# Attention units of a one-core fp32 kernel: VectorE's rescale ahead of the maximum, and masked key blocks left out

## What is computed

```python
# first model, layer 0: four heads of "differential" attention, q and k of 64, v of 128
w = probs(q1b, k1) - lam * probs(q2b, k2)          # softmax(where(causal, s, -inf))
o = einsum('bqhk,bkhd', w, v)
# first model, layer 0: four "forget" heads, a decay added to each score
s = q @ k + cum_logf[query] - cum_logf[key]
o = softmax(where(causal, s, -inf)) @ v
# first model, layer 1: eight heads, three dilated windows (128,1), (512,4), (2048,16),
# merged by their log-sums: one softmax with log(how many patterns hold the key) added
# second model, layer 0: eight query heads over 256 tokens + 256 context keys, no mask
p = softmax(q @ concat(k, k_ctx)); o_ctx = softmax(q_ctx @ k_ctx) @ v_ctx
# second model, layer 1: sixteen heads, blocks of 128 queries
in_window = abs(key - query) <= 128                # of 256 tokens; beyond the edges: no key
s_win = where(in_window & exists, q @ k, -1e30)
p = softmax(concat(s_win, q @ k_ctx, sink))[..., :-1]
```

## Time and profile before

| | |
| --- | --- |
| median of the runs | 2828.0 us (3 runs, 2827.4 to 2834.32) |
| the profiled execution | 2829.54 us, its span 2827.8 us |
| TensorE busy | 2536.1 us, 90% of the span |
| VectorE busy | 1515.0 us, 54% |
| ScalarE busy | 891.9 us, 32% |
| GpSimd busy | 76.5 us, 3% |
| mean granted TensorE clock | 0.951 of full speed |
| DMA | 110 GB/s mean |

### The profile page before, as it was taken

The page is one execution under the profiler, slowest core; times in us unless marked ns, Lnnn a source line. Parts: engine busy times, 40 slices in busy tenths (PEclk is TensorE's granted clock), DMA queues, the critical chain, the costliest instruction groups (busy, mean ns, idle before and its releaser), DMA issues.

```text
span 2827.8 us, 41887 instructions
## 1 busy us (share of the span) xinstructions
PE 2536.1 (90%) x17518; PEld 2006.7 (71%) x17518; DVE 1515.0 (54%) x2517; ACT 891.9 (32%) x1547; POOL 76.5 (3%) x148
## 2 busy tenths in 40 slices
PE   8999999799997899548886899998999997888998
PEld 6687778588875567248773588876788875556998
DVE  5656475555554655674543555545555543664554
ACT  2331131422222333712220422223322223343543
POOL 0000000000000000000000000000000000000000
PEclk9999999999998999779998999999999998999999
DMA  7235436243433110000011243443344441101553
GB/s 285 82 118 200 172 121 220 99 142 135 148 134 136 60 45 31 0 2 4 4 39 52 84 147 137 141 149 119 129 139 142 142 143 69 43 30 45 175 184 134
DMA packets 55770, 309.72 MB, mean 110 GB/s; under 512 B 5920, under 2 KB 9376, under 8 KB 28064
## 3 DMA queue, kind: packets, MB, share of 16 engines
q1 hardware_dynamic: 32944, 224.74, 22.2%
q0 software_dynamic: 20736, 75.51, 8.0%
q10 hardware_dynamic: 1904, 6.80, 0.6%
HBM read 305.98 MB, written 1.05 MB: 109 GB/s over the span
## 4 chain that ended last, share of the span: by engine, by line
PEld 39%; PE 31%; issue 12%; DVE 11%; ACT 7%; DMA 1%; PEldq 0%; DVEq 0%; ACTq 0%; SPq 0%
PEld bank L1206 13%; PEld bank L1199 13%; PEld bank L1202 12%; PE bank L1079 4%; PE bank L1258 4%; PE bank L1076 2%; PE bank L1052 2%; PE bank L1138 2%; PE bank L1154 2%; PE bank L943 2%; PE bank L950 2%; PE bank L946 2%; ACT hn L1567 2%; PEld bank L910 1%; PE bank L1033 1%
## 5 line engine op out<-in xcount | busy, mean ns | idle before, releaser
L1991 DVE TENSOR_TENSOR w_lo<-ring,w_hi 128x1024 fp32r<-128x1024 f32 (+1 forms) x198 | 236.2, 1193 | 450.6 <-ACT w_hi L1532 450.6
L1202 PE MATMUL bank<-ffn_x_lo,w_hi 128*128 128x512 f32 x1008 | 399.6, 396 | 0.0
L1206 PE MATMUL bank<-ffn_x_hi,w_lo 128*128 128x512 f32 x1008 | 399.6, 396 | 0.0
L1199 PE MATMUL bank<-ffn_x_hi,w_hi 128*128 128x512 f32 x1008 | 399.6, 396 | 0.0
L1532 ACT ACTIVATE w_hi<-ring 128x1024 fp32r<-128x1024 f32 (+1 forms) x198 | 203.7, 1029 | 290.2 <-PE bank L1202 278.6
L1923 DVE SCALAR_TENSOR_TENSOR ms<-mod_rows,c_silu 128x1024 f32<-128x1024 f32 x200 | 243.9, 1220 | 1.2
L1206 PEld LDWEIGHTS bank<-ffn_x_hi,w_lo 128*128 128x128 f32 x1008 | 189.9, 188 | 46.3
L1199 PEld LDWEIGHTS bank<-ffn_x_hi,w_hi 128*128 128x128 f32 x1008 | 189.9, 188 | 46.3
L1202 PEld LDWEIGHTS bank<-ffn_x_lo,w_hi 128*128 128x128 f32 x1008 | 189.8, 188 | 46.3
L1199 PE MATMUL bank<-ffn_h_hi,w_hi 128*128 128x512 f32 x528 | 211.7, 401 | 0.0
L1206 PE MATMUL bank<-ffn_h_hi,w_lo 128*128 128x512 f32 x528 | 209.3, 396 | 0.0
(11 more groups left out here) (430 smaller groups left out, 4642.8 us busy)
## 6 DMA issues: line engine op xcount, KB each, us to landing
ring<-in_stream SPq DMA_DIRECT2D x211, 1024.0 KB, 4.8
mod_rows<-in_mod_stream POOLq DMA_DIRECT2D x144, 512.0 KB, 3.8
one_const<-in_one ACTq DMA_DIRECT2D x1, 1665.0 KB, 14.2
mix_const<-in_two ACTq DMA_DIRECT2D x1, 1440.0 KB, 6.2
win_const<-in_win ACTq DMA_DIRECT2D x1, 1089.0 KB, 5.4
x<-in_x SPq DMA_DIRECT2D x4, 256.0 KB, 4.5
c_silu<-in_c SPq DMA_DIRECT2D x1, 1024.0 KB, 10.3
x<-in_x SPq DMA_DIRECT2D x1, 1024.0 KB, 26.5
```

Of the source, the lines that this page charges most:

```text
L1199: mm = pe.matmul(bank[:, 0:tok], w_high, hi, start=k == 0, stop=False)
L1202: mm = pe.matmul(bank[:, 0:tok], w_high, lo, start=False, stop=False)
L1206: mm = pe.matmul(bank[:, 0:tok], w_low, hi, start=False, stop=last)
L1991: V.tensor_tensor(low[:, 0:h.nk, :], raw_half(h), high[:, 0:h.nk, :].bitcast(F32), ALU.subtract).then_inc(sem("w_split"), 1)
```

## The change

It has two parts.

**Key blocks left out.** Units of the first query block (t=0) of the differential, forget and dilated forms now have 128 keys for each part and not 256: half of the score columns, two transposes for four, half of the product matmuls. Window units leave out the block of keys beyond the edge that all of them had in their 512 columns: they have 384. The causal mask is added only on the block of 128 keys on the diagonal (`mask_at`), the window mask only on the 128 token keys that it can shut out in part, the dilated one on all keys that are kept. It is added in place, in PSUM; the tile `s` is not written, the maximum and the exponential read PSUM, and so it is ScalarE that frees the bank, after the exponential, and signals `exp_ready` by an instruction behind that. ScalarE's copy of the transposed probabilities is as wide as the unit.

**VectorE's order.** `step(i)` of VectorE's attention is split into `largest(i)` (mask, maximum, sink, sign) and `rescaled(i)` (the rescale of unit i-1). Where a step follows something other than a unit, `fresh`, `rescaled(i)` comes first: in the mixers always, in the blends in the first step of each group of two or four. In the others the order is as before.

```diff
-                    def step(i):
+                def largest(i):
                     if i < n:
                         u = us[i]
                         bank, free = full_bank()
-                        src = bank[:, 0:u.width]
+                        src = bank[:, 0:u.width].rearrange("p (k w) -> p k w", k=u.parts)
                         if u.mask is not None:
-                            src = u.bufs["s"][:, i % 2, 0:u.width]
-                            link(V.tensor_tensor(src, bank[:, 0:u.width], u.mask, ALU.add))
-                            dve.nop().then_inc(free, 1)
-                        link(V.tensor_reduce(stats[:, i % 4, 0:u.parts], src.rearrange("p (k w) -> p k w", k=u.parts),
-                                             AX_X, ALU.max))
+                            part = src[:, :, u.mask_at:u.mask_at + u.mask.shape[2]]
+                            link(V.tensor_tensor(part, part, u.mask, ALU.add))
+                        link(V.tensor_reduce(stats[:, i % 4, 0:u.parts], src, AX_X, ALU.max))
...
+                def rescaled(i):
                     if 1 <= i < n + 1:
                         u = us[i - 1]
...
+                def step(i, fresh):
+                    if fresh:
+                        rescaled(i)
+                        largest(i)
+                    else:
+                        largest(i)
+                        rescaled(i)
...
 # ScalarE, exponential and copy
-                            src = (u.bufs["s"][:, i % 2, :] if u.mask is not None else psum[b])[:, k * w:(k + 1) * w]
-                            last = nc.scalar.activation(u.bufs["p"][:, i % 3, k * w:(k + 1) * w], src, ACT.Exp,
+                            last = nc.scalar.activation(u.bufs["p"][:, i % 3, k * w:(k + 1) * w], psum[b][:, k * w:(k + 1) * w], ACT.Exp,
...
-                        if u.mask is None:
-                            last.then_inc(bank_free[b], 1)
-                            act.wait_ge(bank_free[b], use + 1)
-                            act.nop().then_inc(sem("exp_ready"), 1)
-                        else:
-                            last.then_inc(sem("exp_ready"), 1)
+                        last.then_inc(bank_free[b], 1)
+                        act.wait_ge(bank_free[b], use + 1)
+                        act.nop().then_inc(sem("exp_ready"), 1)
...
-                        nc.scalar.activation(u.bufs["pT"][:, (i - 2) % 2, :], bank[:, :], ACT.Copy).then_inc(sem("pT_ready"), 1)
+                        nc.scalar.activation(u.bufs["pT"][:, (i - 2) % 2, 0:u.width], bank[:, 0:u.width], ACT.Copy).then_inc(sem("pT_ready"), 1)
...
 # TensorE, transposes
-                        for kt in range(4):
+                        for kt in range(u.width // P):
...
 # units: differential (forget and dilated ones in the same way), window
-                        sc = [(ph1["q"][64 * a:64 * a + 64, h, cols], ph1["q"][64 * a:64 * a + 64, 4 + h, :], SEQ, [])
+                        cols, keys = slice(t * P, (t + 1) * P), (t + 1) * P
+                        sc = [(ph1["q"][64 * a:64 * a + 64, h, cols], ph1["q"][64 * a:64 * a + 64, 4 + h, 0:keys], keys, [])
...
-                            sc = [(ph4["q"][rows, j, cols], ph4["q"][rows, 8 + j // 4, :], TOK, [])]
-                            pv = [(kt, ph4["v"][:, kt, 64 * kv:64 * kv + 64]) for kt in range(4)]
+                            sc = [(ph4["q"][rows, j, cols], ph4["q"][rows, 8 + j // 4, P:TOK], TOK - P, [])]
+                            pv = [(kt, ph4["v"][:, 1 + kt, 64 * kv:64 * kv + 64]) for kt in range(3)]
```

More of the change, by code:

```diff
@@ L59, with __init__ @@
 class Unit:
-    def __init__(self, scores, parts, outs, dst, bufs, mask=None, sink=None, pad=None, minus=False):
+    def __init__(self, scores, parts, outs, dst, bufs, mask=None, mask_at=0, sink=None, pad=None, minus=False):
         self.scores, self.parts, self.outs, self.dst, self.bufs = scores, parts, outs, dst, bufs
-        self.mask, self.sink, self.pad, self.minus = mask, sink, pad, minus
+        self.mask, self.mask_at, self.sink, self.pad, self.minus = mask, mask_at, sink, pad, minus
         self.width = sum(width for _, _, width, _ in scores)
@@ L643, in build, with mask_of @@
                 "pair_w": (c4("perm_pair"), c4("cos2"), c4("sin2"))}
-        def both(a):
-            return a.rearrange("p (t n) -> p t n", t=2)
+        def mask_of(table, t, parts, k0, k1):
+            return table.rearrange("p (t n k) -> p t n k", t=2, n=2)[:, t, 0:parts, k0:k1]
         def units_of(kind):
             us = []
+            if kind in ("diff", "fox", "dilated"):
+                table = c1("dilated" if kind == "dilated" else "causal")
             if kind == "diff":
@@ L664, in units_of @@
                     for t in range(2):
-                        cols = slice(t * P, (t + 1) * P)
+                        cols, keys = slice(t * P, (t + 1) * P), (t + 1) * P
                         sc, outs = [], []
@@ L668, in units_of @@
                             sel = c1("sel").rearrange("p (h n) -> p h n", h=4)[0:4, h, :]
-                            more = [(ph1["cum"][0:4, 1, cols], sel), (sel[:, 0:P], ph1["cum"][0:4, 2, :])]
-                            sc.append((ph1["q"][:, 8 + h, cols], ph1["q"][:, 12 + h, :], SEQ, more))
-                            outs.append((0, P, [(2 * n + kt, ph1["v"][:, kt, (4 + h) * P:(5 + h) * P]) for kt in range(2)]))
-                        us.append(Unit(sc, 2, outs, ph1["o"][:, 4 + 2 * g:6 + 2 * g, cols], mask=both(c1("causal"))[:, t, :], bufs=ph1))
+                            more = [(ph1["cum"][0:4, 1, cols], sel[:, 0:keys]), (sel[:, 0:P], ph1["cum"][0:4, 2, 0:keys])]
+                            sc.append((ph1["q"][:, 8 + h, cols], ph1["q"][:, 12 + h, 0:keys], keys, more))
+                            outs.append((0, P, [(n * (t + 1) + kt, ph1["v"][:, kt, (4 + h) * P:(5 + h) * P]) for kt in range(t + 1)]))
+                        us.append(Unit(sc, 2, outs, ph1["o"][:, 4 + 2 * g:6 + 2 * g, cols], bufs=ph1,
+                                       mask=mask_of(table, t, 2, t * P, keys), mask_at=t * P))
             elif kind == "dilated":
@@ L2059, in blend @@
                 norms, (scores, _) = head_norms(blend_steps(layer)), attention(units)
+                before = None
                 for what, i in blend_order(layer):
@@ L2071, in blend @@
                     elif what == "unit":
-                        scores(i)
+                        scores(i, before != "unit")
                     elif what != "none":
                         norms(what, i)
+                    before = what
             def gated_add(bank, free, layer, v, c, tok):
@@ L2217, in mixer @@
                     elif what == "unit":
-                        scores(i)
+                        scores(i, True)
                     elif what != "silu":
```

17 lines of the change are left out of this document (8 added, 9 removed).

## The result

The changed kernel takes 2847.22 us (median of 4 runs, 2846.53 to 2847.82), the kernel before 2828.07 (4 runs, 2827.4 to 2834.32): a ratio of 1.0058, 95% interval 1.0045 to 1.0071. It is slower by 19 us. The forecast was 2825, and the time lies 9 us above the range.

A forecast was written before the change was run, and what follows sets the result against it. TensorE was taken as busiest, held where chains through VectorE and ScalarE end later. Terms -7.4 - 12.5 + 7.7 + 3.6 + 6 - 0.6 = -3.2 us gave 2826.3, forecast as a 2825 us median; 8-in-10 range 2812 to 2838.

The forecast's parts named there:

- What bounds the kernel, and what the order does: Attention stages: products wait for ScalarE's copy behind the newest exponential; waits reach about 1.7 us (even blend), 2.7 (odd).
- Part 1: Mixers: matmuls left out give -7.4 us, 5.4 in the even and 2.0 in the odd; clock -0.6 more.
- Part 2: Odd blend: narrower units and the 0.44 us mask shorten the chain through VectorE and ScalarE, -12.5 us.
- Part 3: Even blend: rescale ahead of the maximum delays the product by 0.70 us in each of 11 rounds, +7.7 us.
- Part 4: Clock falls after longer waits: odd blend +3.6 us, even blend +6, even mixer -0.6.
- theory W: Experiments' theory: VectorE's new order lengthens TensorE's wait for ScalarE's copy, and the clock falls behind it; order alone 2857 us.
- The slower one: Rival, even blend: the early rescale starves TensorE and its clock falls in all 11 rounds; 2837 us, chance 0.13.
- The clock falls no oftener than now: Rival, blends and even mixer: no added clock falls, -14 us, 2814 to 2816 us; chance 0.29.
- The wait for the rescale is what holds TensorE: Rival, blends and mixers: removing that wait pays, and all matmuls left out count; -41 us, 2787 us, chance 0.03.
- The dear mask: Rival, odd blend: the mask in place costs as much as the full one; +8 us, 2833 us, chance 0.05.

The follow-up runs named there:

- e3: Changed kernel with ScalarE's copy of the transposed probabilities moved ahead of the exponential in every step: 2780.7 us, ratio 0.9834.
- e8: Kernel before with VectorE's new order and ScalarE's copy ahead of the exponential, no key blocks left out: 2814.3 us, ratio 0.9943.
- e7: Kernel before with only ScalarE's copy moved ahead of the exponential: 2815.5 us, ratio 0.9945.
- e2: Changed kernel with VectorE's old order everywhere, key blocks still left out: 2821.4 us, ratio 0.9967.
- e6: Changed kernel with useless matmuls added in the window units: 2843.5 us, ratio 1.0049.
- e5: Changed kernel with VectorE's old order and useless matmuls in the window units, restoring TensorE's old work there: 2802.6 us, ratio 0.9897.
- e1: Kernel before with VectorE's new order alone, no key blocks left out: 2863.0 us, ratio 1.0110.
- e4: Changed kernel with VectorE's old order and ScalarE's copy ahead of the exponential: median 2804.6 us, ratio 0.9908, profiled execution 2787.3 us.
- e12: Same code as e4 (against the changed kernel: old VectorE order, copy ahead of exponential), run again: median 2795.0 us, ratio 0.9877, profiled execution 2803.2 us.

## Why the prediction was wrong

**What bounds the kernel, and what the order does: right.** The prediction said that the product waits for ScalarE's copy, that the copy stands behind the exponential of the newest unit, and that a rescale ahead of the maximum lengthens this wait. The wait was forecast at about 1.7 us in the even blend and 2.7 in the odd one; it is 1.1 to 1.7 and 2.46. The 0.55 us that I took for the wait in each round of the even blend before was one of the longest: the eleven are 0.14 to 0.56. e3 shows the chain from the other side: the copy moved, the wait went. e8 against e7 shows that the order does no harm once the copy is early.

**Part 1, mixers, -7.4 - 0.6: -9.8.** The odd mixer gave 1.9 us where 2.0 were forecast, the even one 7.9 for 6.0. O(1) of the even mixer starts at 121.07 in the changed kernel, for 121.16: 0.1 us earlier, 0.2 were forecast, and its wait grew to 2.12 us. A stretch of 3.4 us at 1.2 GHz came with it (120.9 to 124.3), as the fall that the prediction priced at 1.1 us, and two of the three later ones were gone, where one was forecast to go. What I did not see is how much more there was to have: without the order (e2) the mixers give 16.8, more than the 12.6 us of matmuls, and no stretch at 1.2 GHz is left there, for 10 us before.

**Part 2, odd blend, -12.5: the chain right.** At full clock a round of e2, without the order, took 17.9 us for 20.0, forecast 18.0. The mask took 0.29 us, as the slope said, and the maximum over 384 columns 0.56. In the changed kernel no round ran at full clock, so the 18.8 us with the order can't be read.

The prediction weighed a page of the Trainium skill here: "VectorE: DVE Perf Modes", section "The TRN2 errata", has a fixed term larger by 62 cycles for PSUM than for SBUF. The lines of the changed kernel and of before show none: the maximum of 512 columns had a median of 684 ns from PSUM in its even blend and 686 from SBUF in the odd blend of before. The same section gives N+151 cycles at 0.96 GHz for an fp32 addition of N columns, as measured at 512 and 2048; for 128 columns that makes 291 ns, an estimate, and the mask in PSUM took 299 in the median.

**Part 3, even blend, +7.7: right, a little high.** Of the eight rounds, the seven at full clock took 12.2 us, 0.57 over before, where 0.70 was forecast. With the clock's part the stage came to +13.5; +13.7 was the forecast. That it came so near is in part luck: e6, with the same code there, had +9.4, with 20.5 us at 1.2 GHz in the stage for 27.3.

**Part 4, the clock: this step failed, in the odd blend.** It said: "I take a fall after each of the 6 in the odd blend: 3 more, +3.6 us", each lasting 3.4 us and costing 1.3. That falls come with these waits was right: there is one at each of the five waits of 2.46 us, and the last of them runs on over the place of the sixth. The length was wrong. Four of the stretches are 10.2 to 13.7 us long, and the one that runs through the end part 44.4. In all it is 114 us for 34: 80 more, where three falls of 3.4 make 10.

The price was not what failed. The prediction's 1.3 us for 3.4 is 0.38 for each us at 1.2 GHz. The two executions of one kernel give 0.43, by which the 80 us are 34; e2 against e5 (16.8 us for 71, with the extra matmuls in it) gives 0.24, by which they are 19. The stage lies 22.6 us over its forecast.

I took the length from falls of the kernel before, where the units behind a fall had 512 columns and the waits were 1.7 us. Each half of the change brings long stretches by itself. With the order alone (e1) the waits are 2.8 us, six of the stretches among the units 6.8 to 13.7 long, and the stage costs 21.7 us. With the blocks alone (e2) there are 96 us at 1.2 GHz, and the stage costs 3.3 where theory W, with the clock of before, expected a gain of 16. I held TensorE's work for something that only gets shorter, and did not ask what its clock would do with less work in the same time. The end part was costed at 2.5 us a step, at full clock; at 1.2 GHz its steps take 3.9, and TensorE is the bound there. How the 22.6 us divide between longer waits and narrower units is not shown; e6 gave back 3.3. In the mixers and in the even blend, where the work around the units is dense, the stretches that came with the waits were 3.4 to 6.8 us long and the same reasoning held.

**The rivals.** The slower one was right in sign and wrong in place: it saw the clock fall in all 11 rounds of the even blend, but there it fell in 3, and it gave the odd blend nothing more. "The clock falls no oftener than now" fell. "The wait for the rescale is what holds TensorE" fell with e1: in the odd blend that wait went from 13.9 to 1.6 us, and the kernel took 33 us more. The dear mask fell with its 0.29 us.

## What to carry to other kernels

Before moving a step ahead to serve one waiter, follow the waiter behind it: here the transposes' wait went into the products' one. With ScalarE's copy moved ahead too, both were gone in the even blend, and in the odd one the products' alone; with the blocks left out that kernel is 49 us under the one before. Where TensorE is held by a chain through other engines, matmuls left out of it may cost: price the time at 1.2 GHz too, and try the edit with useless matmuls in place of the old ones, which tells the clock's part from the chain's. Changes that hide each other's effect want all their combinations: the same order of VectorE cost 33 us with one order of ScalarE, and nothing with the other. A stage's figure from one profile is one draw: with the same code it moved by 4 us in the even blend (after, e6) and by 10.7 in the odd one.

## What the runs showed of the hardware

That a kernel gets 19 us faster by useless matmuls (e5 against e2) was not expected, nor that the time at 1.2 GHz in the odd blend differs between executions of one kernel by 25 us, and the stage by 10.7 (e4, e12). Nearly the same idle time did different harm in different pieces: 17.6 us in waits of up to 1.69 us before, with 34 us at 1.2 GHz, and 19.3 us in e1, 16.8 of them in waits of 2.8, with 80. In e2 the clock stayed at 1.2 GHz from 2518.9 to 2563.3 us though TensorE was busy 46.8 of 48.7 us of that end part: at half speed the same work fills the time, so busy time by the profile's page does not show that it has little to do; in e5 the same end part, with more matmuls, had TensorE busy 34.0 of 37.6 us at 2.4 GHz. What the chip goes by was not tested.
